# A normalising product on GpSimd: a per-partition scalar in place of a broadcast second tensor

## What is computed

```
s_own = jnp.where(kpos[None, :] <= qpos[:, None], s_own, NEG)
p = jax.nn.softmax(sc, axis=-1).astype(v.dtype)
...
sc = jnp.where(kpos[None, :] <= qpos[:, None], sc, NEG)
p = jax.nn.softmax(sc, axis=-1).astype(v.dtype)
return jnp.einsum('bhqk,bhkd->bhqd', p, v)
```

## Time and profile before

| | us |
|---|---|
| median of 3 runs | 1271.16 |
| lowest, highest | 1269.46, 1271.94 |
| the profiled execution, whole | 1264.08 |
| its span, first to last instruction | 1262.3 |
| PE busy in it | 1216.9 |
| DVE busy | 831.2 |
| ACT busy | 591.9 |
| POOL busy | 229.5 |

### The profile page before, as it was taken

The page is one execution under the profiler, slowest core; times in us unless marked ns, Lnnn a source line. Parts: engine busy times, 40 slices in busy tenths (PEclk is TensorE's granted clock), DMA queues, the critical chain, the costliest instruction groups (busy, mean ns, idle before and its releaser), DMA issues.

```text
span 1262.3 us, 15586 instructions
## 1 busy us (share of the span) xinstructions
PE 1216.9 (96%) x6036; PEld 1023.4 (81%) x6036; DVE 831.2 (66%) x1178; ACT 591.9 (47%) x889; POOL 229.5 (18%) x208
## 2 busy tenths in 40 slices
PE   6999999989999999999999999999899999999996
PEld 5887777888888888888898787888888888888885
DVE  4698676568666666545669967566676666665463
ACT  4464467445434444434545636655444444444432
POOL 1384276110000000000117726531000000000000
PEclk9999989999999999999999998699999999999998
DMA  7233102533333333556632330035243333336563
GB/s 240 80 85 89 55 1 84 168 117 117 100 91 93 101 100 99 169 193 222 184 85 79 84 94 1 17 134 170 64 117 101 100 90 94 101 100 191 175 230 120
DMA packets 155676, 143.17 MB, mean 113 GB/s; under 512 B 6447, under 2 KB 137427, under 8 KB 155603
## 3 DMA queue, kind: packets, MB, share of 16 engines
q1 hardware_dynamic: 155024, 141.44, 36.6%
q10 hardware_dynamic: 579, 0.74, 0.2%
HBM read 140.07 MB, written 2.10 MB: 113 GB/s over the span
## 4 chain that ended last, share of the span: by engine, by line
PE 80%; DVE 12%; POOL 3%; issue 2%; DMA 1%; ACT 1%; POOLq 0%; DVEq 0%; ACTq 0%
PE ps L472 26%; PE ps L473 25%; PE ps L474 25%; DVE ps L1056 3%; DVE wsp L402 3%; PE ps L686 2%; POOL prob L821 1%; DVE shuf L951 1%; POOL rms_r L779 1%; DVE rot L953 1%; PE ps L532 1%; DVE yt L877 1%; DVE xn L897 1%; DVE hid L958 1%; DMA rows<-in_vectors 1%
## 5 line engine op out<-in xcount | busy, mean ns | idle before, releaser
L472 PE MATMUL ps<-xn,wsp 128*128 128x512 f32 (+2 forms) x1136 | 419.0, 369 | 13.0 <-DVE xn L897 13.0
L473 PE MATMUL ps<-xn,wsp 128*128 128x512 f32 (+2 forms) x1136 | 416.3, 366 | 0.0
L474 PE MATMUL ps<-xn,wsp 128*128 128x512 f32 (+2 forms) x1136 | 416.2, 366 | 0.0
L402 DVE TENSOR_TENSOR wsp<-raw,wsp 128x1024 fp32r<-128x1024 f32 (+2 forms) x250 | 311.0, 1246 | 157.3 <-ACT wsp L394 157.0
L394 ACT ACTIVATE wsp<-raw 128x1024 fp32r<-128x1024 f32 (+1 forms) x256 | 266.9, 1043 | 179.9 <-PE ps L474 149.4
L472 PEld LDWEIGHTS ps<-xn,wsp 128*128 128x128 f32 (+1 forms) x1136 | 215.2, 189 | 50.1 <-DVE xn L897 15.1
L473 PEld LDWEIGHTS ps<-xn,wsp 128*128 128x128 f32 (+1 forms) x1136 | 215.3, 190 | 34.8 <-issue 0.5
L474 PEld LDWEIGHTS ps<-xn,wsp 128*128 128x128 f32 (+1 forms) x1136 | 215.2, 189 | 34.8
L472 PE MATMUL ps<-wsp,hid 128*128 128x512 f32 (+1 forms) x488 | 189.7, 389 | 0.0
L474 PE MATMUL ps<-wsp,hid 128*128 128x512 f32 (+1 forms) x488 | 189.1, 388 | 0.0
L473 PE MATMUL ps<-wsp,hid 128*128 128x512 f32 (+1 forms) x488 | 189.0, 387 | 0.0
(11 more groups left out here) (137 smaller groups left out, 1380.2 us busy)
## 6 DMA issues: line engine op xcount, KB each, us to landing
raw<-in_w_ffn_up SPq DMA_DIRECT2D x88, 512.0 KB, 3.8
raw<-in_w_ffn_down SPq DMA_DIRECT2D x88, 512.0 KB, 3.8
raw<-in_w_in SPq DMA_DIRECT2D x40, 512.0 KB, 3.9
raw<-in_w_out SPq DMA_DIRECT2D x32, 512.0 KB, 3.5
x<-in_x SPq DMA_DIRECT2D x4, 512.0 KB, 8.1
out_x<-x SPq DMA_DIRECT2D x4, 512.0 KB, 4.2
raw<-in_w_uq SPq DMA_DIRECT2D x4, 288.0 KB, 3.0
gain_mix<-in_norm_mix_post SPq DMA_DIRECT2D x2, 512.0 KB, 5.0
```

The lines of the kernel that those rows point to most:

```text
L402: eng.tensor_tensor(wsp[:, u % SPLIT, 1, 0:nk * n], raw[:, (l * NU + u) % RAW, 0:nk * n], fp(wsp[:, u % SPLIT, 0, 0:nk * n]), ALU.subtract ...
L472: pe.matmul(dst, a[0], b[0], start=start, stop=False, skip_group_check=True)
L473: pe.matmul(dst, a[0], b[1], start=False, stop=False, skip_group_check=True)
L474: return pe.matmul(dst, a[1], b[0], start=False, stop=stop, skip_group_check=True)
```

## The change

The product on POOL is the same, element by element. Before, `rowinv[:, t:t+1]` was spread to n columns as the second tensor of a two-tensor instruction; now it is the scalar operand, one value for each partition, of an instruction with one tensor input. The 64 instructions, their places in POOL's queue, their waits and their signals stay; the queues of PE, DVE, ACT and SP are the same.

```
-                    pool.tensor_tensor(prob[:, t % NPROB, 0:n], prob[:, t % NPROB, 0:n],
-                                       rowinv[:, t:t + 1].to_broadcast([P, n]), ALU.mult).then_inc(prob_done, 1)
+                    pool.tensor_scalar(prob[:, t % NPROB, 0:n], prob[:, t % NPROB, 0:n], rowinv[:, t:t + 1], None,
+                                       ALU.mult).then_inc(prob_done, 1)
```

## The result

The changed kernel takes 1274.79 us in the median of 20 runs (1267.06 to 1278.74), the kernel before 1267.95 us in the median of 20 (1259.37 to 1272.59). The ratio is 1.0052 with a 95% interval of 1.0032 to 1.0072: by the ratio 6.6 us slower, 4.1 to 9.1. My number was 1267, my range ended at 1279, my chance for slower was 0.26. The forecast was wrong in its sign; what came is rival 1. That the time still fell inside my range says nothing for the forecast: the range was drawn to take in nearly all of rival 1.

What follows compares the result with a forecast made beforehand. PE was near its bound in both attention stages, POOL counting only where PE idled for its product. Savings of 2.87 us (first layer) and 1.83 (second) made 4.7, cut to 4: 1271.16 - 4 = 1267 us, range 1259 to 1279.

Steps and rivals of the forecast that it cites:

- rival 1: POOL's product is dearer, above 1.04 us at 512 columns; 8.6 us slower in both stages, 1279.8 us; chance 0.25.
- The price of the instruction: POOL's product at L821 would take 0.29, 0.40, 0.51 and 0.62 us at the four widths.
- the low end: Price of POOL's product from the select and the fills: 0.62 us at 512 columns, saving 0.42.
- the high end: Price of POOL's product from L770's elementwise row: 0.55 to 1.65 us, an excess of 0.15 to 0.61.
- What lies on the path: Attention stages' start, a few single tiles, tiles after weight splits, drain: savings of 2.87 us first layer, 1.83 second.
- The size of the gain: Both attention stages: 4.7 us summed, 4 us expected; below 3.7 if each scalar read costs 85 ns.
- the next late thing: After a wait on POOL, PE's queue or DVE's mask comes next; a little under a fifth off 4.7 us.
- Rival 3: Attention stages' clock: staying high gives 1251 or 1259 us, chance 0.11; the other way 1276 us, chance 0.03.
- What would show it right or wrong: Profile checks: L821 near 0.3 and 0.6 us; PE's idle time for it from some 5 us to 1 or less.

Runs made afterwards that it cites:

- the 11 tiles: Kernel before, with the one-operation scalar form only at tiles 2, 3, 14, 15, 16, 19, 20, 23, 24, 30, 31: ratio 1.0018, 7.0 us slower at equal clock.
- the 21 others: Kernel before, with the one-operation scalar form only at the 21 tiles not taken for those without slack: ratio 1.0004, 2.6 us slower at equal clock.
- the narrow products: Kernel before, with the one-operation scalar form only at 128 and 256 columns: ratio 0.9973, 3.6 us slower at equal clock.
- the row of prices: Kernel before plus POOL instructions on scratch, three of each form, each waiting for the one before: at 512 columns 1.62 us one operation, 0.76 two, 1.09 broadcast.

## Why the prediction was wrong, step by step

**The price of the instruction** is the step that failed. I took the low end, 0.62 us at 512 columns, "because the select is of the same family, reads and writes one tensor as the new instruction does". It measured 1.56 us; at 128, 256 and 384 columns 0.60, 0.92 and 1.24 in most tiles. That is near the high end of 0.55 to 1.65 us drawn from L770. The fill, the copy and the scalar form with two operations all go at 0.84 ns a column, the scalar form with one at 2.5 [(1562 - 600) / 384]. The family told nothing, for within the same instruction the absence of a second operation doubles the time at 512 columns (1.63 against 0.76). The Trainium skill's rule (GPSIMD Engine Reference, section 4.1, one-input work at roughly line rate) holds for the copy at 0.65 us and the two-operation form, not for the form that this change used. No row before told the two apart; the choice of one end there was a guess, and with the ends 2.6 times apart the low end should have had no more than an even chance, where I left the high one 0.25.

**What lies on the path** was right in the main: the start of each stage, the tiles behind the weight splits, the drain. Rival 1's working with the measured excess (0.20, 0.31, 0.42, 0.52 us) gives 1.45 + 0.42 + 3 x 0.72 + 0.52 = 4.6 us in the first layer and 0.42 + 0.52 + 0.42 + 2 x 0.72 + 0.52 = 3.3 in the second, 7.9 in all. Measured at equal clock: 9.2 +- 0.7; the 11 tiles by themselves 7.0, the 21 others 2.6. Part of the 2.6 is tile 10, which was one of my places. In the drain I had missed the wait at tile 30: from the start of its product to the end of tile 31's the changed kernel took 2.78 us where the one before took 2.14, so 0.64 for my 0.52. And the narrow products lost 3.6 where these places give 1.5; why, no run shows.

**The size of the gain**, had the price been right, was too large: 3.7 us by my sum for the two-operation form's prices, 1.9 +- 0.7 measured. I took off a little under a fifth for the next late thing; it was half, and I had named DVE's mask where PE's new wait is on DVE's low part.

**Rival 1** gave 1279.8 us from the old median of 3 runs, which lay 3.2 us above that of 20. Its mechanism, its place and its point of decision (above 1.04 us at 512 columns) came true. Its 8.6 us belong to equal clock; 2.7 of the 9.2 were given back by the clock. Why a slower POOL leaves the plain kernel a slightly higher mean clock is not settled; the profiles show long stretches at 1.2 GHz in one stage or the other in either kernel.

**Rival 3**, the clock, was right in that it moves times by 10 us and more from run to run, and wrong in that this change hardly moves it in this kernel. The matmuls put into PE's idle time show that the idle time at the start alone was not the lever.

**What would show it right or wrong** named this outcome: a 512 of L821 above 1.04 us brings rival 1, and it read 1.56. PE's idle time for it rose from 6.1 to 12.0 us in place of falling; the "some 5 us" of the prediction left out tile 30.

## What to carry to other kernels

On GpSimd a float32 product with a per-partition scalar was cheap here only with both operations of the instruction written out, times 1.0 in second place; price the exact form in a row of three on scratch before rewriting. Of a dearer instruction on a side engine it is mainly the places without slack that count: list the waits that end on it one by one, and ask of a gain what is late next. Where run times spread with the granted clock, compare kernels at equal clock before arguing from 0.3%, and look for changes that keep the clock up: here they were worth more than the instruction.

## What the runs showed that I had not expected

- One-tensor product on POOL, 128x512 float32: 1.56 us with one operation, 0.69 with two, 1.04 with the scalar spread as a second tensor, 0.65 for a copy.
- A scalar column costs about 0.08 us an instruction.
- Beside DVE's feed-forward work the 512-wide groups of the row of prices read higher, the 128-wide ones hardly. The group of three with one operation took 8.29 us there against 4.87 at the end, the one with a constant 5.09 against 4.63. In the attention stages the one-operation form kept to its price, but for tiles 4 and 5 of each, which took 1.03 and 1.37 us beside DVE's `cf_out` products.

```profile
921.47 8.29 POOL L803 TENSOR_SCALAR rope_c<-rope_c,ones 128x512 f32<-128x512 f32 x3
```

- 84 runs of one kernel fall on a line of 0.97 us for each 0.001 of mean granted clock. With the transposes as products, two kernels that differ in nothing but a written-out "times 1.0" on POOL lie 27 us apart, 2.2%, with 6 runs each.
